# Layer 1 of a two-layer decoder step: key pages as product and reduction, later key blocks and position bias added by VectorE, masks ahead of pages

## The reference, cut to what matters

```python
z = einsum('bqhd,bshd->bhqs', q, k) * d ** -0.5 + offset     # q, k RMS-normed
log_rest = where(k_pos < q_pos, log_sigmoid(-z), 0)
between  = cumsum(log_rest, axis=3, reverse=True) - log_rest  # over later keys
weight   = where(k_pos < q_pos, exp(log_sigmoid(z) + between), 0)
oc = einsum('bhqs,bshd->bqhd', weight, v) * silu(gate)
mixed = einsum('gts,bnsgc->bntgc', tril(w_s), vn) + b_s[t]    # position bias b_s
od = u * mixed * silu(gate)
```

## Time and profile before

| | |
|---|---|
| median of 3 runs | 2234.89 us (2234.24 to 2239.43) |
| the profiled execution: its own time | 2237.85 us |
| its span | 2236.3 us |
| TensorE matmul busy | 2116.0 us (95%) |
| VectorE busy | 1156.1 us (52%) |
| ScalarE busy | 605.5 us (27%) |
| mean DMA rate | 199 GB/s |
| mean granted TensorE clock | 0.974 |

### The profile page before, as it was taken

One profiled execution on the slowest core, in us unless ns is written; L12 is line 12 of the kernel. 1 busy time (PEld: TensorE's weight loads), 2 busy tenths in 40 slices (PEclk: granted clock), 3 DMA queues, 4 the chain that ended last, 5 costly groups with the idle time before them and its releaser, 6 DMA issues.

```text
span 2236.3 us, 45304 instructions
## 1 busy us (share of the span) xinstructions
PE 2116.0 (95%) x16847; PEld 1868.0 (84%) x16847; DVE 1156.1 (52%) x3617; ACT 605.5 (27%) x773; POOL 200.5 (9%) x319
## 2 busy tenths in 40 slices
PE   6789999999999999899789998999999999999997
PEld 2268888898888888899789996888888888888997
DVE  1543544435445356544452576776677677635332
ACT  1322222222121222322233423233232323324221
POOL 0000101101011011000000011111111111000110
PEclk9989999999999999999899999999999999999999
DMA  9977666566665766343422467798798788763441
GB/s 322 304 229 233 194 185 199 181 209 202 194 206 181 221 185 188 104 116 110 161 84 85 127 208 232 260 298 273 246 300 266 253 287 274 237 181 104 131 134 57
DMA packets 401524, 444.97 MB, mean 199 GB/s; under 512 B 17268, under 2 KB 307406, under 8 KB 399807
## 3 DMA queue, kind: packets, MB, share of 16 engines
q1 hardware_dynamic: 359270, 311.99, 45.4%
q0 software_dynamic: 32288, 122.12, 15.8%
q10 hardware_dynamic: 9810, 8.73, 1.2%
HBM read 416.18 MB, written 26.61 MB: 198 GB/s over the span
## 4 chain that ended last, share of the span: by engine, by line
PE 82%; DVE 9%; ACT 3%; DMA 3%; issue 3%; SPq 0%; DVEq 0%; ACTq 0%; POOLq 0%
PE pt L548 65%; PE m L548 15%; DVE arena L1733 2%; PE m L552 2%; ACT w_hi L971 2%; ACT arena L971 1%; DMA raw<-in_e_w_ada 1%; DVE w_lo L1349 1%; DMA arena<-in_o_k_norm_g 1%; PE pt L552 1%; DVE arena L1897 1%; DVE arena L1787 0%; DMA arena<-in_cache_k 0%; DVE arena L1468 0%; DVE act_lo L1429 0%
## 5 line engine op out<-in xcount | busy, mean ns | idle before, releaser
L548 PE MATMUL pt<-act_hi,w_hi 128*128 128x260 f32 x4384 | 911.9, 290 | 41.7 <-DVE w_lo L1349 13.3
L548 PE MATMUL pt<-act_hi,w_lo 128*128 128x260 f32 x4384 | 891.0, 285 | 0.0
L548 PE MATMUL pt<-act_lo,w_hi 128*128 128x260 f32 x4384 | 889.3, 285 | 0.0
L1349 DVE TENSOR_TENSOR w_lo<-raw,w_hi 128x1024 fp32r<-128x1024 f32 x274 | 335.7, 1225 | 850.3 <-ACT w_hi L971 849.3
L548 PEld LDWEIGHTS pt<-act_hi,w_hi 128*128 128x128 f32 x4384 | 683.7, 191 | 105.3 <-issue 85.4
L548 PEld LDWEIGHTS pt<-act_lo,w_hi 128*128 128x128 f32 x4384 | 684.5, 191 | 0.0
L548 PEld LDWEIGHTS pt<-act_hi,w_lo 128*128 128x128 f32 x4384 | 684.0, 191 | 0.0
L971 ACT ACTIVATE w_hi<-raw 128x1024 fp32r<-128x1024 f32 x274 | 289.9, 1058 | 1156.9 <-PE pt L548 1139.6
L1733 DVE CUSTOM_DVE_ANT_0 arena<-arena 128x128 f32<-128x128 f32 x1024 | 223.9, 287 | 44.6 <-DMA arena<-in_cache_k 44.0
L971 ACT ACTIVATE arena<-arena 128x1040 f32<-128x1040 f32 (+8 forms) x191 | 158.1, 837 | 192.9 <-DVE arena L1833 75.5
L548 PE MATMUL m<-raw,cond 128*9 128x512 f32 x768 | 130.1, 638 | 18.7 <-DMA raw<-in_e_w_ada 16.5
(11 more groups left out here) (169 smaller groups left out, 1135.5 us busy)
## 6 DMA issues: line engine op xcount, KB each, us to landing
arena<-in_cache_k POOLq DMA_DIRECT2D x128, 512.0 KB, 5.0
arena<-in_cache_v SPq DMA_DIRECT2D x128, 512.0 KB, 5.1
raw<-in_o_w_in SPq DMA_DIRECT2D x112, 512.0 KB, 5.7
raw<-in_e_w_in SPq DMA_DIRECT2D x98, 512.0 KB, 4.5
raw<-in_e_w_ada SPq DMA_DIRECT2D x96, 512.0 KB, 5.9
raw<-in_o_w_ada SPq DMA_DIRECT2D x96, 512.0 KB, 5.3
raw<-in_e_w_out SPq DMA_DIRECT2D x32, 512.0 KB, 3.9
raw<-in_o_w_out SPq DMA_DIRECT2D x32, 512.0 KB, 4.7
```

The lines of the kernel that those rows point to most:

```text
L548: return pe.matmul(out, lhsT, rhs, start=start, stop=stop, skip_group_check=True)
L1349: tt(w_lo[:, b, :], raw[:, sl, :], w_hi[:, b, :].bitcast(F32), ALU.subtract)\
```

## The change

Six edits, all in layer 1. (1) A key page is no longer eight fused product-and-sum instructions, one for each head, but one product over 128x1024, in place, and one `tensor_reduce` over it. (2) VectorE adds up later key blocks into `above`, so that `between` takes 768 columns of `ones` matmuls in place of 1280. (3) The position bias is broadcast over the partitions by a transfer (`head_bias`, behind page 3 on GpSimd's queue) and added by VectorE in `gate`; the four single-row matmuls are gone. (4) `rest` and its masks come ahead of pages 8 and 9 in step 7, and the masks of `weight` ahead of pages 12 and 13 in step 9. (5) `pick` goes from step 1 to step 2, behind the sums over later pages, and writes to another bank; `rows_picked` goes from step 1 to step 3. (6) The semaphore counts follow. The additions to the counts of the chain of steps are 16 for the pages, two for the sums, one for the bias (38 for two passes).

```diff
         orow = z[:, 0:256]
+        above = tmp[1][:, 0:384]
         eps = sb("eps", [P, 1])
...
                 for e in range(2):
-                    last = mm(M[3][:, 384 + 4 * e:388 + 4 * e], orow[:, P * e:P * e + P],
+                    last = mm(M[2][:, 384 + 4 * e:388 + 4 * e], orow[:, P * e:P * e + P],
                               cm["pick"][:, 4 * e:4 * e + 4])
...
                 yield
-                if not first:
-                    pick(i)
                 yield
...
                 mm(M[3][:, 256:376], ones[:, :], later, start=False, stop=True).then_inc(s("s_sum"), 1)
+                if not first:
+                    pick(i)
                 yield
...
                     pe.wait_ge(s("gated"), i)
-                pe.wait_ge(s("ws_in"), i * 32 + 32)
+                pe.wait_ge(s("ws_in"), i * 16 + 16)
                 mm(M[0], ones[:, :], tmp[0][:, 0:T])
                 mm(M[1][:, 0:8], ones[:, :], tmp[0][:, T:N])
+                pe.wait_ge(s("vn"), i + 1)
                 tr(M[2][:, 0:P], ws)
-                pe.wait_ge(s("vn"), i + 1)
                 tr(M[2][0:NB, P:2 * P], tmp[2][:, T:N]).then_inc(s("p0"), 1)
...
                               start=True, stop=(b == 3))
-                    for l in range(b + 1, NT):
-                        last = mm(m012[:, off + P * (l - b):off + T - P * b], ones[:, :],
-                                  za[:, SB_OFF[l]:SB_OFF[l] + T - P * l], start=False, stop=(l == 3))
+                    for at, x in (((P, za[:, 512:640]), (2 * P, above[:, 128:384])),
+                                  ((P, za[:, 1024:1152]), (2 * P, above[:, 0:128])), ((P, za[:, 896:1024]),), ())[b]:
+                        last = mm(m012[:, off + at:off + at + x.shape[1]], ones[:, :], x, start=False, stop=True)
                 last.then_inc(s("between"), 1)
...
                 for t in range(NT):
-                    mm(M[1][:, P * t:P * t + P], vntok[:, t, :], wst, start=True, stop=False)
-                    last = mm(M[1][:, P * t:P * t + P], ones[0:1, :], brow[0:1, 0:P], start=False, stop=True)
+                    last = mm(M[1][:, P * t:P * t + P], vntok[:, t, :], wst)
                 last.then_inc(s("oc"), 1)
...
                 if p == 0:
-                    dve.wait_ge(s("qb"), b * 16 + 16)
+                    dve.wait_ge(s("qb"), 16 if isinstance(b, int) and b == 0 else b * 32)
                 slot = key_slot(p)
                 dve.wait_ge(s(f"page{slot}"), b * 128 + 16 * (p // 2 + 1))
-                for h in range(HC):
-                    kpage = pages[:, slot, P * h:P * h + P]
-                    last = dve.tensor_tensor_reduce(kpage, kpage, qb[:, P * h:P * h + P], 1.0, 0.0,
-                                                    ALU.mult, ALU.add, to[:, 8 * p + h:8 * p + h + 1])
-                last.then_inc(s("k_free"), 1)
+                kpage = pages[:, slot, :]
+                step(tt(kpage, kpage, qb, ALU.mult))
+                dve.tensor_reduce(to[:, HC * p:HC * p + HC], kpage.rearrange("p (h d) -> p h d", h=HC),
+                                  mybir.AxisListType.X, ALU.add).then_inc(s("k_free"), 1)
...
                 copy(OS[:, :, bass.ds(n - 1, 1)].rearrange("p (q e) b -> p e (q b)", e=2),
-                     M[3][:, 384:384 + HC].rearrange("p (e q) -> p e q", e=2)).then_inc(s("mixed1"), 1)
+                     M[2][:, 384:384 + HC].rearrange("p (e q) -> p e q", e=2)).then_inc(s("mixed1"), 1)
...
                 dve.wait_ge(s("oc"), n)
-                tt(to[:, 0:T], G[4][:, 0:T], M[1], ALU.mult)
+                dve.wait_ge(s("qb"), 32 * HC if isinstance(n, int) and n == HC else n * 32 + 16)
+                step(tt(tmp[3][:, 0:T].rearrange("p (t k) -> p t k", t=NT), M[1].rearrange("p (t k) -> p t k", t=NT),
+                        brow[:, 0:P].unsqueeze(1).to_broadcast([P, NT, P]), ALU.add))
+                tt(to[:, 0:T], G[4][:, 0:T], tmp[3][:, 0:T], ALU.mult)
                 tt(wide[:, bass.ds(hd, 1), 0:T].rearrange("p c n -> p (c n)"), G[2][:, 0:T], M[0], ALU.mult)\
...
                 yield
-                if not first:
-                    rows_picked(i)
                 dve.wait_ge(s("zs_l"), i + 1)
...
                 if not first:
+                    rows_picked(i)
                     dve.wait_ge(s("gated"), i)
...
                 yield
-                keys(7)
                 dve.wait_ge(s("z_l"), i + 1)
                 step(stt(za, z, 0.0, za, ALU.max, ALU.add))
-                masks(za).then_inc(s("rest"), 1)
+                step(masks(za))
+                tt(above[:, 128:256], za[:, 640:768], za[:, 1024:1152], ALU.add)
+                step(tt(above[:, 0:128], za[:, 1152:1280], za[:, 896:1024], ALU.add))
+                tt(above[:, 256:384], za[:, 768:896], above[:, 0:128], ALU.add).then_inc(s("rest"), 1)
+                keys(7)
                 yield
...
                 tt(z, z, m012[:, 0:SB_ALL], ALU.subtract).then_inc(s("lw"), 1)
-                keys(9)
                 dve.wait_ge(s("w_e"), i + 1)
                 masks(za).then_inc(s("weight"), 1)
+                keys(9)
                 yield
...
             with dve.Fori(0, 3) as n:
-                step.body(n, 0, 24)
+                step.body(n, 0, 62)
                 l1b(n * 2 + 1, 1)
                 l1b(n * 2 + 2, 0)
-            step.end(3, 24)
+            step.end(3, 62)
             l1b(7, 1, True)
...
                 pool.dma_start(ws, a["o_w_s"][0, bass.ds(h, 1)].rearrange("g t s -> t (g s)")).then_inc(s("ws_in"), 16)
-                pool.dma_start(brow[0:1, 0:P], a["o_b_s"][0, bass.ds(h, 1)]).then_inc(s("ws_in"), 16)
+
+            def head_bias(h):
+                if not (isinstance(h, int) and h == 0):
+                    pool.wait_ge(s("gated"), h)
+                    pool.sem_inc(s("pool_waited"), 1)
+                if not (isinstance(h, int) and h == HC - 1):
+                    pool.wait_ge(s("qb"), h * 32 + 32)
+                    pool.sem_inc(s("pool_waited"), 1)
+                pool.dma_start(brow[:, 0:P], a["o_b_s"][0, bass.ds(h, 1), :].rearrange("b n -> (b n)")
+                               .partition_broadcast(P)).then_inc(s("qb"), 16)
...
                             pool.wait_ge(s("q_out"), 16)
+                        if not (isinstance(b, int) and b < 2):
+                            pool.wait_ge(s("qb"), b * 32 - 16)
+                            pool.sem_inc(s("pool_waited"), 1)
                         queries(b)
...
                             head_weights(b - 1)
+                    if p == 3 and not (isinstance(b, int) and b == 0):
+                        head_bias(b - 1)
...
             head_weights(HC - 1)
+            pool.wait_ge(s("qb"), 32 * HC - 16)
+            head_bias(HC - 1)
```

## The result

The changed kernel takes 2303.02 us (median of 4 runs, 2300.08 to 2306.43) against 2235.68 us for the kernel before (4 runs beside it). The ratio is 1.0298, 95% interval 1.0282 to 1.0314: 3% slower. The profiled execution took 2302.8 us with a span of 2301.3. Three executions among those run beside the experiments (2625 and 7080 us of the kernel before, 2947 of `e15_both`) were in a slow state and count in no ratio.

What follows compares the result with a forecast made beforehand. TensorE bounds the kernel before at about 83 us a pass, VectorE the changed one at 89.2. 2237.85 + 33.3 (seven cycles) + 4.2 (start) - 2.5 (last pass) = 2272.9, stated as 2270 us; 8-in-10 range 2246 to 2286.

Steps and rivals of the forecast that it cites:

- Part 1, the page: Key page as one product and one reduction on VectorE: 2.40 us in place of 1.70, +11.2 us a pass.
- Part 2, fewer matmuls: TensorE: four bias matmuls fewer, -1.67 us a pass, `between` -0.87; its pass goes from 83.0 to about 80.5 us.
- Part 3: VectorE: bias addition +0.72 us a pass, three additions into `above` +0.8; the bias transfer on GpSimd's queue costs nothing.
- Part 4: Pages moved behind the masks: TensorE gets masks 3.4 us earlier; VectorE's open wait for ScalarE's Exp costs +1.4 us.
- The step that failed: Key page loads: transfers move along with the moved pages, so VectorE's waits of 5.3 us a pass stay about the same.
- The sum as a contest of two bounds: Each pass: VectorE's cycle becomes 89.2 us against TensorE's 80.5, so VectorE sets the pass; chance 0.80.
- 8 us of VectorE "to spare": Kernel before, each pass: VectorE's own cycle of 75.1 us is hidden under TensorE's 83, about 8 us to spare.
- Start and end: Ahead of the seven cycles, in `l1a`, six pages at 0.70 add +4.2 us; the last pass, TensorE-bound, gives -2.5.
- The third: Rival: transfers land later or VectorE also waits for a late TensorE, +2.5 us a cycle, 2288 us; chance 0.07.
- The first: Rival: TensorE stays the bound at 80.5 us a pass, 2216 us; needs a page of at most 1.86; chance 0.08.
- The second: Rival: bounds come out close, page transfers hide under longer products, cycle 83.9 us, about 2233 us, no change; chance 0.05.
- What the profile was to show: Reduction 1.1 to 1.25 us, VectorE 73 busy, `w_hi` waits about 8, TensorE idle 5 or more at L1842 or L1848.

Runs made afterwards that it cites:

- e15_both: Kernel before with later key blocks added up by VectorE and one bias matmul over 512 columns in place of four: 2236.4 us, ratio 0.9988.
- e4_halfreduce: Changed kernel with the reduction over only the first four heads (512 elements), a page of 1.87 us: 2272.59 us (one run).
- e13_orderquarter: Changed kernel with fused key pages, pages 8, 9, 12, 13 in their old places and a quarter of each key page loaded: 2213.54 us (one run).
- e14_beforequarter: Kernel before with only a quarter of each key page loaded: 2231.47 us (one run).
- e11_onebias: Kernel before with one bias matmul over 512 columns on TensorE in place of four: 2237.33 us, ratio 0.9998.
- e5_order: Changed kernel with fused key pages and pages 8, 9, 12, 13 back in front of the masks: 2250.03 us, ratio 1.0055.
- e9_bias: Kernel before with only the position bias moved to VectorE (broadcast transfer, addition in `gate`): 2254.88 us, ratio 1.0068.
- e6_moves: Kernel before with only the pages moved, 8 and 9 behind the mask of `rest`, 12 and 13 behind that of `weight`: 2247.53 us, ratio 1.0048.
- e12_fusedquarter: Changed kernel with fused key pages and only a quarter of each key page loaded: 2237.64 us (one run).
- e1_fused: Changed kernel with the key page as before, eight fused product-and-sum instructions: 2266.54 us, ratio 1.0132.
- e18_three_after: Changed kernel with the five page buffers split three for keys and two for values, in place of two and three: 2276.2 us (one run).
- e3_quarter: Changed kernel with only a quarter of each key page loaded and a maximum in place of the page's product: 2268.4 us (one run).
- e16_three_e5: Kernel of e5_order with three page buffers for keys and two for values, in place of two and three: 2225.53 us, ratio 0.9956.
- e2_pages: Kernel before with only the key page changed to one product and one reduction: 2301.1 us, ratio 1.0273.

## Why the prediction was wrong, step by step

The direction was right and so was the reckoning of VectorE's work. The size was 30 us short in the profiled execution (2302.8 against 2272.9): 26.3 in the seven cycles, 3.2 ahead of them, 0.5 behind.

**Part 1, the page.** Right: the reduction lasts 1.22 us, the page 2.40. The Trainium skill, "VectorE: DVE Perf Modes", section "The perf-mode tier table", has `tensor_reduce` at the single rate only, and the trace agrees: 1.22 us for 1024 elements, like the two-input product, not the 0.70 of the fp32 copy. A reduction at the copy's rate would not have saved the forecast, though: at a page of 1.87 us `e4_halfreduce` is at 2272.6, not 2216.

**Part 2, fewer matmuls.** The price was about right: TensorE is busy for 79.3 us a cycle in `e13_orderquarter` and 82.2 in `e14_beforequarter`, 2.9 less where I said 2.5. The effect was not: `e11_onebias` and `e15_both` gain nothing with two key buffers.

**Part 3.** The additions' price was about right: `e5_order`, which has them, keeps VectorE busy for 61.4 us a cycle, 1.2 more than before, where I said 1.5. That the bias as a whole would be cheap (0.72 us of VectorE, its transfer at nothing, 1.67 us less of TensorE) failed: `e9_bias` loses 15 us against the kernel before.

**Part 4.** The open wait for Exp is 9.4 / 7 = 1.34 us, forecast 1.4. As a price for the whole move that is not one number: alone it is 8.6 us over the seven cycles (`e6_moves`), 1.2 each and near the forecast; on top of parts 2 and 3 the medians say 16.5 us in all, the two profiled executions only 6.1 in the cycles; with quick loads it is 24 us (`e12_fusedquarter` less `e13_orderquarter`, one run each), 3.5 a cycle. Where it costs more, the traces show another end of it. Pages 12 and 13 and, as their buffers come free later, the loads of 14 and 15 go to the end of the pass, in front of the sample's `s_rest`, for which TensorE stops: 42.1 us in the cycles of `e1_fused`, 16.6 in those of `e5_order`. `e1_fused`, end of one pass, VectorE's timeline (thinned) and the start of TensorE's stop:

```profile
1592.22 0.90 DVE L1787 TENSOR_TENSOR arena<-arena,c_below 128x128 f32<-128x128 f32 x4 [1.34 <-ACT arena L971]
...
1603.10 0.29 DVE L1733 CUSTOM_DVE_ANT_0 arena<-arena 128x128 f32<-128x128 f32 x1 [4.15 <-DMA arena<-in_cache_k]
...
1606.05 0.29 DVE L1733 CUSTOM_DVE_ANT_0 arena<-arena 128x128 f32<-128x128 f32 x1 [1.17 <-DMA arena<-in_cache_k]
...
1610.41 0.29 DVE L1835 SCALAR_TENSOR_TENSOR mod<-mod,per_head 128x128 f32<-128x128 f32 x1 [2.57 <-issue]
...
1615.94 1.23 DVE L1349 TENSOR_TENSOR w_lo<-raw,w_hi 128x1024 fp32r<-128x1024 f32 x1 [4.58 <-ACT w_hi L971]
```

```profile
1617.42 0.80 PE L549 MATMUL m<-arena,c_from_key 128*128 128x128 f32 x2 [5.88 <-DVE arena L1843]
```

Read down: masks, two late pages (4.15 and 1.17 us of waiting for loads that pages 12 and 13 let go), then the next pass's first instruction (behind a jump back here, 2.57 us), then ScalarE, and TensorE has stood for 5.88 us.

**The step that failed** is this one: "The transfers move along with the pages: a page's load starts when the page two before is read, so these waits of 5.3 us stay about as they are." They became 10.1 us a cycle. Its reason says when a load starts, not how late it lands against the page that needs it. The account of a cycle, forecast and measured: busy 73.3 and 71.6; `w_hi` 8.2 and 8.4; Exp 1.4 and 1.3; key pages 5.3 and 10.1; jump back 1.4 and 0.6; the rest 1.0 and 2.3. Sum 90.6 and 94.4 (94.3 by the rounded terms); the pages are the one large difference. `e18_three_after` takes these waits away (22.8 / 7 = 3.3) and has a cycle of 90.9, with a time of 2276.2. `e3_quarter`, with quick loads, has 90.4.

Which pages are waited for, in the seven cycles (sums in us, added up from VectorE's timelines; `e1_fused` has 0.8 more at page 13):

| | pages 4 to 7 | of it page 7 | pages 10 and 11 | pages 14 and 15 |
|---|---|---|---|---|
| before | 12.4 | 0 | 12.6 | 14.5 |
| changed | 38.6 | 24.5 | 17.1 | 14.9 |
| e5_order | 44.1 | 19.9 | 11.1 | 15.1 |
| e9_bias | 49.9 | 22.1 | 17.5 | 17.3 |
| e1_fused | 19.8 | 3.5 | 34.0 | 29.0 |

So in the changed kernel it is hardly the loads that moved with the pages: 10, 11, 14 and 15 wait 4.9 us more in all, over seven cycles. The growth is at pages 4 to 7, which stand where they stood, and 24.5 of the 31 us are at page 7 alone, which was never waited for before. The sum has no term for that.

Two causes can be read from the traces. One is plain latency in a loop: a load starts only when its buffer is read, and lands 4 to 9 us later, so where the steps between come sooner the wait gets longer (`e11_onebias` +26 us, `e4_halfreduce` +15). The other is where the load falls among SyncE's. A page 7 in the changed kernel (issues of GpSimd and SyncE, and VectorE's start):

```profile
1575.07 1.50 SPq L466 DMA_DIRECT2D arena<-in_cache_v  x2
1576.16 0.53 POOL L1986 DMA_DIRECT2D arena<-in_cache_k  x1 [3.59 <-DVE mod L1733]
1576.93 0.38 SPq L368 DMA_DIRECT2D raw<-in_o_w_in  x1
...
1585.12 1.22 DVE L1732 TENSOR_TENSOR arena<-arena 128x1024 f32<-128x1024 f32 x1 [5.58 <-DMA arena<-in_cache_k]
```

The same page of the same pass in the kernel before:

```profile
1545.89 0.53 POOL L1982 DMA_DIRECT2D arena<-in_cache_k  x1 [1.31 <-DVE mod L1733]
1548.36 1.50 SPq L465 DMA_DIRECT2D arena<-in_cache_v  x2
...
1552.21 0.28 DVE L1733 CUSTOM_DVE_ANT_0 arena<-arena 128x128 f32<-128x128 f32 x1
```

Behind two value pages of SyncE it takes 1585.12 - 1576.16 = 9.0 us; ahead of them it is there within 6.3, as page 6 is done, and nobody waits for it. The other passes agree. In six of the seven cycles of the changed kernel the value pages are issued 0.7 to 2.2 us ahead of page 7's load, which then lands after 5.7 to 9.1 us and is waited for. In the remaining one, the first, they are issued 3.2 us behind it, and in all seven cycles of before 2.2 to 3.1 us behind it, and page 7 is not waited for. That is what goes together in the traces; no run moves SyncE's issues alone, so the collision as the cause is likely but not shown. The median over all key pages is even shorter after (4.6 us from issue to landing, 5.0 before), so transfers are not slower in general.

A total of page waits is not a price by itself. `e6_moves` has 90.5 us of them, more than the changed kernel, and is at 2247.5: what VectorE waits for pages there it waits less for `w_hi` (71.7 us in place of 115.4). In the changed kernel the waits for `w_hi` are down to 8.4 us a cycle, about the 8.2 that are VectorE waiting for its own results, and nothing is left to take up a page that comes late.

**The sum as a contest of two bounds.** "The order turns round: VectorE sets the pass" is half the truth, and its counterpart, 8 us of VectorE "to spare" before, is what `e1_fused` (+31 where -20 was due) and `e4_halfreduce` refute. A pass is one loop through both engines. TensorE ends a unit, ScalarE and VectorE split the next; `between` goes to VectorE, to ScalarE's Exp, to the masks, which release pages, whose buffers release loads. Waits on either side can then add instead of hiding behind the larger sum. TensorE's stops also make its own work longer. Three windows of the changed kernel: before one stop of 6.63 us for `s_rest`, from its end at 1547.4, and a little later (the third number from the end is the granted clock):

```profile
1536.00:1540.00 4.00, 4.00 (x36) 4.00 (x35) 2.52 (x3) 0.00 (x0) 0.53 (x1) 1.00 0.63 203
1547.40:1551.50 4.10, 3.60 (x15) 3.31 (x16) 3.93 (x9) 0.00 (x0) 0.00 (x0) 0.50 0.46 132
1554.00:1558.00 4.00, 4.00 (x44) 3.40 (x42) 3.59 (x9) 1.01 (x2) 0.53 (x1) 1.00 0.64 228
```

The granted clock is 1.00, then 0.50, then 1.00: of the two levels, 2.4 and 1.2 GHz, it is the lower one for some 4 us behind the stop. With the same matmuls TensorE is busy for 79.7 us a cycle in `e16_three_e5` (granted clock 1.00 in most cycles), 81.7 in `e5_order` (0.94 to 0.98) and 83.8 in the changed kernel (0.93 to 0.96). The changed kernel has a stop for `s_rest` in every pass, `e16_three_e5` in two. Some of the 4 us between the two can be matmuls missing from the trace (669 a cycle are listed in `e16_three_e5`, 680 in the changed kernel). They are more than the 2.5 us that the change took out, which fits with TensorE's busy time having risen; as TensorE is idle for 10.6 us of the cycle, they alone do not set its length.

**Start and end.** The start was +7.4 against +4.2, the end -2.0 against -2.5. The extra 3 us at the start go with the page and its loads: the first pass starts at 1348.1 with the page alone (`e2_pages`), at 1337.7 without it (`e1_fused`), and at 1342.8 with it and quick loads (`e3_quarter`).

**The rivals.** The third (transfers land later, or VectorE waits for TensorE, 2288) was nearest and 15 us short as well. Its first half is right for page 7 and not for the median, its second is not seen: the waits for `w_hi` stayed at 8.4. The first is met only by `e13_orderquarter`, a kernel without the slow page and the move, with a quarter of the bytes. The second needed the page waits gone, and they grew.

**What the profile was to show.** The reduction of 1.22 us, `w_hi` waits of 8, and TensorE's idle at L1842 of 6.4 us a cycle on average (44.9 / 7) came as said, but for one pass of the eight with 2.8. VectorE is busy 71.6 where 73 was said. Waits for the masks did not go: 1.9 us before, 21.4 after. The page waits did not vanish, but that they could double was on no list.

## What to carry to other kernels

Before two engines' times are compared as two bounds, see whether a loop runs through both: then a saving on one is worth something only up to the first load or result that the loop waits for, and small waits on both sides add up. For a double-buffered stream, write down for each load when its buffer comes free, when it is needed and how long it takes to land; a step moved between these two moves the load as well. Do that for every load of the loop, not only for those whose step moves. A buffer more, or a quarter of the bytes, tells in one run whether the loads are what holds the loop.

## What the runs showed of the hardware

- Eight fused product-and-sum instructions of 128 columns (0.21 us a start, 1.70 a page) beat one product and one reduction over the same 1024 columns (2.40), with an accumulator read for each of the eight.
- The 512 KB load of key page 7 landed 5.7 to 9.1 us after its issue where SyncE's two value pages of 512 KB each had been issued 0.7 to 2.2 us ahead of it (six cycles of the changed kernel); the median over all key pages is 4.6 us.
- Behind a stop of TensorE of 6.63 us the granted clock was 0.50 for some 4 us, then 1.00 again.
- The idle of VectorE at the two jumps back went from 9.8 to 4.5 us in the changed kernel, whose VectorE runs 1857 instructions in all; in `e1_fused`, with the eight instructions of the old page and 3649 in all, it was 4.9 as well, so their number is not what sets it. What does stays open.
